# Where the tiles lie in SBUF: large buffers at multiples of 1024 bytes, small ones last

## The chip, the cores and the metric

One NeuronCore of a Trainium2 chip runs the whole program in one launch. The metric is the device time of one execution in microseconds (us). The median of three runs of the kernel before is 3648.97 us (3647.49 to 3654.26).

## What is computed

Two blocks follow each other on 256 tokens of width 1024, all in fp32. The first has two layers of feed-forward (SwiGLU, inner width 2816), a mixer and a second feed-forward. The mixer joins a causal depthwise convolution (31 taps) and differential attention with 4 heads. The second block has one retention mixer, one gated spatial unit, and behind each of them a "PEER" layer: 8 heads pick 16 of 16,384 experts for each token. This is the core of the reference, cut to the parts that carry the time:

```
x = x + 0.5 * swiglu(rms_norm(x, g1), w_gate, w_up, w_down)      # 1024 -> 2816 -> 1024
a, g, q, k, v = split(rms_norm(x, g2) @ w_in)                    # mixer
x = x + concatenate([conv(a, g), diff_attention(q, k, v)]) @ w_out
...
x = x + g1 * retention_mixer(h, ...)      # layer 0 of the second block
x = x + g1 * sgu_mixer(h, ...)            # layer 1 of it
x = x + g2 * peer_ffn(h, ...)             # both layers
# peer_ffn: scores of h @ w_query against sub_keys, top 16 of 128 twice, top 16 of the 256 sums,
#   softmax gates; u = expert_u[idx]; a = gelu(u . x) * gate; out = a . expert_v[idx]
return rmsnorm(x, norm_final)
```

## The kernel before

The activations lie transposed: 8 tiles of 128 channels by 256 tokens. Every large product is done in three passes, since a factor in the matmul's `float32r` type loses bits: each factor is split into a high part (`h_hi`, `w_hi`, `a_hi`, ...) and a low part (the rest, `h_lo`, `w_lo`, ...), and TensorE adds high*high, low*high and high*low. The three are the lines 548, 549 and 550 (`triple`), and 553, 554 and 555 (`loose`, for the PEER layers' second product). The first operand of each call is the stationary one, the 128x128 block that is loaded into the array; the second is the moving one, 256 columns of 4 bytes, or 1024 bytes in each partition. In `project_rows` the roles are swapped and 512 columns of weights move.

The weights stream from HBM. SyncE issues one transfer of 1 MB per pair of "units" into one of three `raw` buffers; for each unit (128x1024) ScalarE writes `w_hi` (line 936), VectorE (line 1316) or, for the PEER queries and first expert table, GpSimd (line 1892) writes `w_lo`, and TensorE uses the pair in 24 matmuls. Four unit slots of `w_hi` and `w_lo` rotate. The order of the work on each engine is written out by hand, and semaphores tie them.

What moves in a matmul is one of these: a slice of `h_hi` or `h_lo`, 256 columns (projections, 3 x 4416 matmuls); a tile of the "arena", whose names are `at...` in the trace, 256 columns (second products, 3 x 1152 at lines 548 to 550, and 3 x 2048 at 553 to 555); or a slice of `w_hi`/`w_lo`, 512 columns (3 x 192).

The partition is filled from the front by `sb`, one buffer behind the other at multiples of 32 bytes. The arena is one large buffer; `place` puts tiles into it at a given offset, and `carve` one behind the other. 16,512 bytes are taken before the first buffer. From the sizes in the code the start of each buffer follows, and its rest when divided by 1024:

```
buffer                      before      rest    after       rest
x                           16512       128     17408       0
h_hi, h_lo                  24704 ...   128     25600 ...   0
raw (3 x 8192 bytes)        51904       704     41984       0
w_hi, w_lo (4 x 4096)       76480 ...   704     66560 ...   0
arena                       109248      704     99328       0
a_hi, rc_hi, z_hi, p_hi...  in arena    704     in arena    0
mixer's cat_hi, cat_lo      in arena    160     in arena    0
```

The tiles of the second row from below lie at multiples of 1024 bytes within the arena already; slices of 256 tokens within any of these keep the rest of the whole. The weights' blocks of 128 columns (512 bytes) start at a rest of 704 or 192 before, and of 0 or 512 after.

Of the kernel before, what the change touches and what calls it, by code (L numbers as in the profile page):

```python
# [9 lines left out]
FR = mybir.dt.float32r  # L10
# [7 lines left out]
T = 256  # L18
# [4 lines left out]
UNIT = 1024  # L23
BLK = 8
NRAW = 3
NPAIR = 4
NEG = -1e30
NRING = 38
NLATE = 5
NI = 32  # L30
# [63 lines left out]
def carver(place, at=0):  # L94

    state = [at]

    def take(*shape, dt=FP):
        v = place(state[0], *shape, dt=dt)
        n = int(np.prod(shape))  # L100
        state[0] += (n if dt is not HF else (n + 1) // 2) + 7 & ~7
        return v

    return take, state


def weight_order(a):
# [3 lines left out]
    def add(key, src, count, lo="v", n0=0):  # L111
        nonlocal n
        for i in range(n0, n0 + count):
            first.setdefault(key, n) if n0 == 0 and i == 0 else None
            order.append((src[i], lo, n))
            place[key, 2 * i], place[key, 2 * i + 1] = n, n + 1
            n += 2
# [19 lines left out]
    def add_peer(l):  # L137
        u, v = a["peer_u"][l], a["peer_v"][l]
        for i in range(8):
            add(("peer_q", l), a["peer_q"][l], 1, "p", i)  # L140
            if i >= 1:
                add(("peer_u", l), u, 1, "p", i - 1)
        add(("peer_u", l), u, NRING // 2 - 7, "p", 7)
        for i in range(64):
            add(("peer_v", l), v, 1, "v", i)
            if i + NRING // 2 < 64:
                add(("peer_u", l), u, 1, "p", i + NRING // 2)

# [12 lines left out]
def build(nc, a, out):  # L161
    ctx = ExitStack()
    with ctx:
        def sb(name, shape, dt=FP):
            return ctx.enter_context(nc.sbuf_tensor(name, shape, dt))[:]

        def signal(name, order=lambda: 1):
            return Signal(ctx.enter_context(nc.semaphore(name)), order)

        x = sb("x", [128, KT, T])  # L170
        hh_ = sb("h_hi", [128, KT, T], FR)
        hl_ = sb("h_lo", [128, KT, T], FR)
        sq = sb("sq", [128, 2, T])
        tmp_h = sb("tmp_h", [128, 3, T])
        ident = sb("ident", [128, 128])
# [10 lines left out]
        gs = sb("gs", [128, L, 16])  # L186
        lam = sb("lam", [128, 20])
        subg = sb("subg", [128, L])
        raw_t = sb("raw", [128, NRAW, 2 * UNIT])
        whi = sb("w_hi", [128, NPAIR, UNIT], FR)  # L190
        wlo = sb("w_lo", [128, NPAIR, UNIT], FR)
        NA = 29000
        arena_at = (nc.sbuf_base + 31) // 32 * 32
        sb("arena", [128, NA])

        def place(at, *shape, dt=FP):
            n = int(np.prod(shape))
            assert at % 8 == 0 and at + (n if dt is not HF else (n + 1) // 2) <= NA
            v = nc.alloc_sbuf_tensor_at(f"at{at}_{nc.next_id()}", [128, n], dt, offset=arena_at + 4 * at)[:]
# [13 lines left out]

        A_BIAS = NA - 4 * 384
        A_TRI = A_BIAS - D - 3 * T
# [225 lines left out]
        carve, end = carver(place)  # L441
# [4 lines left out]
        carve, end = carver(place)  # L446
# [8 lines left out]
        msqa = [carve(2, T) for _ in range(4)]  # L455
        mrs = [carve(2 * T) for _ in range(2)]
        mdiag = [carve(128) for _ in range(4)]
        cat_hi, cat_lo = carve(8, T, dt=FR), carve(8, T, dt=FR)
        msg = [carve(2, T) for _ in range(2)]
        mct = [carve(T) for _ in range(2)]  # L460
# [9 lines left out]
        carve, end = carver(place)  # L470
# [14 lines left out]
        carve, end = carver(place)  # L485
# [14 lines left out]
        carve, end = carver(place)  # L500
        G = [carve(NI // 2, T) for _ in range(3)]
        scratch_end = end[0]
        R = carve(NRING, T)
        p_hi = [carve(T, dt=FR) for _ in range(4)]
# [8 lines left out]
        carve, end = carver(place)  # L513
# [30 lines left out]
        def _(e):  # L544
# [288 lines left out]
            def peer(l):  # L833
# [4 lines left out]
                def u_pair(n):  # L838
                    b = take(ub, ("u", l, n))
                    project(q, unit[("peer_u", l), 2 * n], b[:, 0:T])  # L840
                    project(q, unit[("peer_u", l), 2 * n + 1], b[:, T:2 * T])

                n_u = 0
                for n in range(8):
# [12 lines left out]
                    if n >= 1:  # L857
                        u_pair(n_u)
                        n_u += 1
                for n in range(n_u, NRING // 2 - NLATE):  # L860
                    u_pair(n)
# [15 lines left out]

                late = list(range(NRING // 2 - NLATE, NRING // 2))
                for gg in range(16):
# [1168 lines left out]
```

## Time and profile before

| | |
|---|---|
| median of 3 runs | 3648.97 us |
| the profiled execution | 3643.59 us, span 3641.8 us, mean granted clock 0.951 |
| TensorE matmul busy | 3387.4 us (93%), 28,708 matmuls |
| TensorE weight load busy | 3304.4 us (91%) |
| VectorE busy | 2338.4 us (64%) |
| ScalarE busy | 1668.5 us (46%) |
| GpSimd busy | 847.6 us (23%) |
| moved by DMA | 588.31 MB, mean 162 GB/s |

How to read it: a matmul's busy time runs from its start to its modelled end, and neighbours overlap; so the time that one takes out of the stream is the distance from its start to the next start, which the timeline shows, and not its duration. The granted clock is the share of TensorE's full 2.4 GHz; 0.5 is 1.2 GHz.

### The profile page before, as it was taken

The page shows a single profiled execution, that of the slowest core. Times are in us where ns is not written, and L with a number is a line of the kernel's source. Part 1 is how long each engine was busy: PE and PEld are TensorE (multiplying, and loading weights), DVE is VectorE, ACT ScalarE, POOL GpSimd, SP SyncE. Part 2 cuts the span into 40 slices and gives each one's busy share as a digit, 9 for nine tenths or more (in the row PEclk, how much of TensorE's full clock was granted, in tenths as well). Part 3 has the DMA queues.
Part 4 walks back from the last instruction along what each step waited for, and adds up shares of the span by engine and source line. Part 5 has one row for each costly group of instructions (what it writes and reads, how often), then busy time and mean ns, then how long its engine had stood idle before and what let it go on. Part 6 is the DMA issues. An engine that isn't in the chain of part 4 may idle for free.

```text
span 3641.8 us, 66194 instructions
## 1 busy us (share of the span) xinstructions
PE 3387.4 (93%) x28708; PEld 3304.4 (91%) x28708; DVE 2338.4 (64%) x3670; ACT 1668.5 (46%) x2556; POOL 847.6 (23%) x421
## 2 busy tenths in 40 slices
PE   7996899997799998989999999999987999999999
PEld 7985799996699898979999999989987999999998
DVE  5766586867477655984554736666589546465565
ACT  5444454544544454434444444456443344444444
POOL 0014000006000001662334343000066233433310
PEclk9998899998899999978999999999998799999999
DMA  6651366663166443433445354445444253544433
GB/s 225 232 215 52 119 252 224 252 219 127 55 217 248 174 151 139 151 116 123 156 144 181 129 176 148 151 173 181 163 141 138 82 176 137 174 141 161 163 131 124
DMA packets 82656, 588.31 MB, mean 162 GB/s; under 512 B 9308, under 2 KB 10912, under 8 KB 11712
## 3 DMA queue, kind: packets, MB, share of 16 engines
q1 hardware_dynamic: 80064, 575.70, 45.0%
q10 hardware_dynamic: 1888, 6.94, 0.5%
q8 instruction: 227, 3.72, 0.4%
q0 software_dynamic: 416, 1.45, 0.2%
q14 instruction: 61, 0.50, 0.0%
HBM read 583.00 MB, written 1.05 MB: 160 GB/s over the span
## 4 chain that ended last, share of the span: by engine, by line
PE 80%; DVE 14%; ACT 4%; issue 1%; DMA 0%; ACTq 0%; DVEq 0%
PE ps L548 16%; PE ps L549 16%; PE ps L550 16%; PE ps L875 7%; PE ps L553 7%; PE ps L555 7%; PE ps L554 7%; PE ps L676 2%; DVE at L1726 1%; DVE at L1777 1%; PE ps L600 1%; DVE at L1807 1%; DVE w_lo L1316 1%; ACT w_hi L936 1%; DVE at L1474 1%
## 5 line engine op out<-in xcount | busy, mean ns | idle before, releaser
L936 ACT ACTIVATE w_hi<-raw 128x1024 fp32r<-128x1024 f32 x1000 | 1055.6, 1058 | 851.5 <-PE ps L550 633.3
L1316 DVE TENSOR_TENSOR w_lo<-raw,w_hi 128x1024 fp32r<-128x1024 f32 x712 | 893.2, 1258 | 645.1 <-ACT w_hi L936 644.5
L548 PE MATMUL ps<-h_hi,w_hi 128*128 128x256 f32 x4416 | 1257.1, 285 | 47.7 <-POOL w_lo L1892 33.4
L549 PE MATMUL ps<-h_lo,w_hi 128*128 128x256 f32 x4416 | 1243.9, 282 | 0.0
L550 PE MATMUL ps<-h_hi,w_lo 128*128 128x256 f32 x4416 | 1242.5, 281 | 0.0
L1892 POOL TENSOR_TENSOR w_lo<-raw,w_hi 128x1024 fp32r<-128x1024 f32 x288 | 722.8, 2517 | 1759.8 <-ACT w_hi L936 1759.8
L548 PEld LDWEIGHTS ps<-h_hi,w_hi 128*128 128x128 f32 x4416 | 853.4, 193 | 55.2 <-POOL w_lo L1892 33.8
L549 PEld LDWEIGHTS ps<-h_lo,w_hi 128*128 128x128 f32 x4416 | 854.2, 193 | 0.8 <-issue 0.2
L550 PEld LDWEIGHTS ps<-h_hi,w_lo 128*128 128x128 f32 x4416 | 852.4, 193 | 0.0
L553 PE MATMUL ps<-at,w_hi 128*128 128x256 f32 x2048 | 591.3, 289 | 8.4 <-DVE at L1826 8.4
L555 PE MATMUL ps<-at,w_lo 128*128 128x256 f32 x2048 | 582.6, 284 | 0.0
L554 PE MATMUL ps<-at,w_hi 128*128 128x256 f32 x2048 | 582.6, 284 | 0.0
L553 PEld LDWEIGHTS ps<-at,w_hi 128*128 128x128 f32 x2048 | 398.2, 194 | 9.0 <-issue 9.0
L554 PEld LDWEIGHTS ps<-at,w_hi 128*128 128x128 f32 x2048 | 396.0, 193 | 0.0
L555 PEld LDWEIGHTS ps<-at,w_lo 128*128 128x128 f32 x2048 | 395.7, 193 | 0.0
L548 PE MATMUL ps<-at,w_hi 128*128 128x256 f32 x1152 | 334.1, 290 | 6.6 <-DVE at L1555 3.7
L549 PE MATMUL ps<-at,w_hi 128*128 128x256 f32 x1152 | 328.0, 285 | 0.0
L550 PE MATMUL ps<-at,w_lo 128*128 128x256 f32 x1152 | 327.9, 285 | 0.0
L875 PE MATMUL ps<-at,at 128*128 128x32 f16 x4096 | 293.2, 248 | 14.1 <-DVE at L1807 14.0
L875 PEld LDWEIGHTS ps<-at,at 128*128 128x128 f16 x4096 | 275.7, 163 | 21.0 <-issue 16.4
L1826 DVE TENSOR_TENSOR at<-at,at 128x256 fp32r<-128x256 f32 x256 | 97.6, 423 | 290.8 <-ACT at L1252 290.8
L1801 DVE TENSOR_TENSOR at<-at,at 128x2048 f16<-128x2048 f16 x128 | 209.3, 1635 | 38.4 <-PE ps L875 38.3
(252 smaller groups left out, 3522.6 us busy)
## 6 DMA issues: line engine op xcount, KB each, us to landing
raw<-in_peer_u SPq DMA_DIRECT2D x128, 1024.0 KB, 4.9
raw<-in_peer_v SPq DMA_DIRECT2D x128, 1024.0 KB, 4.9
raw<-in_ffn_gu SPq DMA_DIRECT2D x88, 1024.0 KB, 4.8
raw<-in_ada_w SPq DMA_DIRECT2D x48, 1024.0 KB, 4.8
raw<-in_ffn_down SPq DMA_DIRECT2D x44, 1024.0 KB, 4.8
raw<-in_w_in SPq DMA_DIRECT2D x16, 1024.0 KB, 4.8
raw<-in_peer_q SPq DMA_DIRECT2D x16, 1024.0 KB, 4.9
raw<-in_sgu_v SPq DMA_DIRECT2D x12, 1024.0 KB, 4.8
```

The costliest lines, as they stand in the source:

```text
L548: e.matmul(o, lhs[0], rhs[0], start=start, stop=False)
L549: e.matmul(o, lhs[0], rhs[1], start=False, stop=False)
L550: return e.matmul(o, lhs[1], rhs[0], start=False, stop=stop)
L553: e.matmul(o, lhs[0], rhs[0], start=start, stop=False, skip_group_check=True)
L554: e.matmul(o, lhs[0], rhs[1], start=False, stop=False, skip_group_check=True)
L555: return e.matmul(o, lhs[1], rhs[0], start=False, stop=stop, skip_group_check=True)
L875: t = e.matmul(b[:, k * NI:(k + 1) * NI], Bh[j][:, :, k], Ah[j][:, z, :, k], start=z == 0, stop=z == 1)
L936: e.activation(whi[:, u % NPAIR, :], raw(k, half), ACT.Copy).then_inc(hi_done.hit(u), 1)
L1316: e.tensor_tensor(wlo[:, m % NPAIR, :], raw(k, half), whi[:, m % NPAIR, :].bitcast(FP), ALU.subtract).then_inc(w_lo_dve.hit(m), 1)
L1801: e.tensor_tensor(Bh[j], jT[:, t0:t0 + 16].unsqueeze(1).broadcast_to([128, 128, 16]), iot, ALU.is_equal)
L1826: e.tensor_tensor(p_lo[k % 4], R[:, ir + e2, :], p_hi[k % 4].bitcast(FP), ALU.subtract).then_inc(p_lo_done.hit(l, k), 1)
L1892: e.tensor_tensor(wlo[:, n % NPAIR, :], raw(k, half), whi[:, n % NPAIR, :].bitcast(FP), ALU.subtract).then_inc(w_lo_pool.hit(n), 1)
```

## The change

No instruction is added, removed or moved: on each engine the same operations with the same tiles and shapes stand in the same order. Only addresses differ. A filler of 896 bytes brings the first buffer to a multiple of 1024; `raw`, `w_hi`, `w_lo` and the arena move in front of the small buffers (all of them whole multiples of 1024 bytes long but the arena, which is last of them); and the mixers' concatenated tiles are carved at the next multiple of 256 floats. The small buffers (`sq`, `tmp_h`, `ident`, `ones`, `cols`, `rr` and so on) now follow the arena, from byte 215,328 on.

```
+LINE = 1024
...
+        front = -((nc.sbuf_base + 31) // 32 * 32) % LINE
+        if front:
+            sb("front", [128, front], mybir.dt.uint8)
         x = sb("x", [128, KT, T])
         hh_ = sb("h_hi", [128, KT, T], FR)
         hl_ = sb("h_lo", [128, KT, T], FR)
+        raw_t = sb("raw", [128, NRAW, 2 * UNIT])
+        whi = sb("w_hi", [128, NPAIR, UNIT], FR)
+        wlo = sb("w_lo", [128, NPAIR, UNIT], FR)
+        NA = 29000
+        arena_at = (nc.sbuf_base + 31) // 32 * 32
+        assert arena_at % LINE == 0, (arena_at, front)
+        sb("arena", [128, NA])
         sq = sb("sq", [128, 2, T])
         tmp_h = sb("tmp_h", [128, 3, T])
...
         subg = sb("subg", [128, L])
-        raw_t = sb("raw", [128, NRAW, 2 * UNIT])
-        whi = sb("w_hi", [128, NPAIR, UNIT], FR)
-        wlo = sb("w_lo", [128, NPAIR, UNIT], FR)
-        NA = 29000
-        arena_at = (nc.sbuf_base + 31) // 32 * 32
-        sb("arena", [128, NA])
...
         mdiag = [carve(128) for _ in range(4)]
+        carve, end = carver(place, -(-end[0] // T) * T)
         cat_hi, cat_lo = carve(8, T, dt=FR), carve(8, T, dt=FR)
```

## Rows read from the trace of the kernel before

**Rows 1.** Page, busy time: share of the span and instructions of each engine.

```profile
PE 3387.4 (93%) x28708; PEld 3304.4 (91%) x28708; DVE 2338.4 (64%) x3670; ACT 1668.5 (46%) x2556; POOL 847.6 (23%) x421
```

**Rows 2.** Page, costliest groups: busy us, mean ns | idle before, releaser.

```profile
L548 PE MATMUL ps<-h_hi,w_hi 128*128 128x256 f32 x4416 | 1257.1, 285 | 47.7 <-POOL w_lo L1892 33.4
...
L553 PE MATMUL ps<-at,w_hi 128*128 128x256 f32 x2048 | 591.3, 289 | 8.4 <-DVE at L1826 8.4
...
L548 PE MATMUL ps<-at,w_hi 128*128 128x256 f32 x1152 | 334.1, 290 | 6.6 <-DVE at L1555 3.7
```

**Rows 3.** Timeline, TensorE, first to second PEER product: start us, us; clock 1.0.

```profile
1719.73 0.28 PE L550 MATMUL ps<-h_hi,w_lo 128*128 128x256 f32 x1
...
1721.77 0.28 PE L550 MATMUL ps<-h_hi,w_lo 128*128 128x256 f32 x1
1721.88 0.28 PE L553 MATMUL ps<-at,w_hi 128*128 128x256 f32 x1
...
1723.91 0.28 PE L555 MATMUL ps<-at,w_lo 128*128 128x256 f32 x1
```

**Rows 4.** Timeline, TensorE, clock 1.0: w_out at 408 us, ffn_down at 550 us.

```profile
407.74 0.28 PE L549 MATMUL ps<-at,w_hi 128*128 128x256 f32 x1
...
408.21 0.28 PE L550 MATMUL ps<-at,w_lo 128*128 128x256 f32 x1
...
549.76 0.28 PE L549 MATMUL ps<-at,w_hi 128*128 128x256 f32 x1
...
550.96 0.28 PE L550 MATMUL ps<-at,w_lo 128*128 128x256 f32 x1
```

**Rows 5.** Timeline, TensorE, retention's rows: moving w, 512 columns, clock 1.0.

```profile
1262.03 0.39 PE L548 MATMUL ps<-w_hi,h_hi 128*128 128x512 f32 x1
...
1263.86 0.39 PE L550 MATMUL ps<-w_hi,h_lo 128*128 128x512 f32 x1
```

**Rows 6.** Timeline, TensorE, around 620 and 978 us, clock 0.5.

```profile
619.92 0.41 PE L548 MATMUL ps<-h_hi,w_hi 128*128 128x256 f32 x1
...
621.42 0.41 PE L549 MATMUL ps<-h_lo,w_hi 128*128 128x256 f32 x1
...
978.09 0.41 PE L550 MATMUL ps<-at,w_lo 128*128 128x256 f32 x1
...
979.80 0.41 PE L549 MATMUL ps<-at,w_hi 128*128 128x256 f32 x1
```

**Rows 7.** Timeline, TensorE, a two-pass fp32 product, clock 1.0; its groups row.

```profile
99.57 1.88 PE L647 MATMUL ps<-at,at 128*128 128x512 f32 x4
...
L682 PE MATMUL ps<-at,half 128*128 128x512 f32 x16 | 8.2, 591 | 0.0
```

**Rows 8.** Windows by stage, line 548 alone: us, PE busy (x), clock, DMA share, GB/s.

```profile
1400.00:1535.00 135.00, 87.06 (x300) 0.94 0.44 151
1535.00:1680.00 145.00, 60.71 (x198) 0.78 0.28 95
1680.00:2380.00 700.00, 199.22 (x720) 1.00 0.46 157
...
2755.00:2900.00 145.00, 60.44 (x196) 0.78 0.28 95
```

**Rows 9.** Windows by stage: us, PE, PEld, DVE, ACT, POOL, clock, DMA share, GB/s.

```profile
400.00:530.00 130.00, 126.99 (x1092) 126.83 (x1092) 97.71 (x142) 66.97 (x98) 0.00 (x0) 0.97 0.64 234
530.00:598.00 68.00, 68.00 (x580) 68.00 (x579) 45.77 (x61) 31.77 (x43) 0.00 (x0) 1.00 0.65 235
...
1535.00:1680.00 145.00, 121.06 (x1138) 119.39 (x1137) 113.93 (x170) 49.53 (x85) 63.27 (x25) 0.78 0.28 95
1680.00:2380.00 700.00, 693.91 (x6542) 691.43 (x6542) 398.85 (x490) 309.44 (x468) 220.09 (x88) 1.00 0.46 157
```

**Rows 10.** One line's instructions: duration ns min/median/max; DMA issues, us to landing.

```profile
L1892 POOL TENSOR_TENSOR w_lo<-raw,w_hi x288: 2361/2407/3515, 1417.4 to 3489.7; 128x1024 fp32r<-128x1024 f32 x144
...
raw<-in_ffn_gu SPq DMA_DIRECT2D x88, 1024.0 KB, 4.8
```

**Rows 11.** Page, costliest groups: split of the weights on VectorE.

```profile
L1316 DVE TENSOR_TENSOR w_lo<-raw,w_hi 128x1024 fp32r<-128x1024 f32 x712 | 893.2, 1258 | 645.1 <-ACT w_hi L936 644.5
```

## The prediction

> **What bounds the kernel now.** First the page: TensorE's matmuls are busy for 3387.4 us of the 3641.8 us span, 93%; VectorE comes next with 64% [rows 1]. Then the cut by stages: in the second feed-forward product TensorE is busy for 68.00 of 68 us, in the long PEER stretch for 693.91 of 700, while VectorE is at 67% and 57% there and the DMA engines at 0.65 and 0.46 [rows 9]. Where TensorE waits, it is short in sum (47.7 us ahead of line 548's 4416 matmuls, 8.4 us ahead of line 553's [rows 2]). So in most of the span nothing but TensorE's own stream sets the time, and the question is what one matmul takes out of that stream.
>
> That is read from starts in the timeline. With `h` as the moving operand, 18 slots lie between 1719.73 and 1721.77: 113.3 ns each. Right behind them, with an arena tile moving against the same weight buffers, 17 slots lie between 1721.88 and 1723.91: 119.4 ns [rows 3]. In the feed-forward it is 10 slots in 1.20 us, 120 ns; with the mixer's concatenated tiles 4 slots in 0.47 us, 117.5 ns [rows 4]. With 512 columns of weights moving, 8 slots in 1.83 us, 228.8 ns [rows 5]. 256 columns at 2.4 GHz are 106.7 ns and 512 are 213.3: each wide matmul pays 6.6, 10.8, 13.3 or 15.5 ns on top. At half clock, 7 slots in 1.50 us and 8 in 1.71 us are 214 ns each, for `h` and for the concatenated tiles alike, against 213.3 for 256 columns at 1.2 GHz [rows 6]. So what comes on top isn't a fixed part of the instruction; it shows only when the columns are read at the full rate, and it depends on which buffer moves.
>
> Beside the addresses it has an order: a start with a rest of 128 by 1024 costs 6.6 ns, 160 costs 10.8, 704 (192 by 256 or by 512) costs 13.3. Counted in cycles of 2.4 GHz that is 272, 282 and 288; with the starts taken by 256, 128, 160 and 192 bytes are 32, 40 and 48 elements, and 240 plus that count gives 272, 280 and 288. Three points on a line, and at rest 0 the line would be under the 256 cycles that the columns need. The stationary blocks start at 704 or 192 in all but the 512-column case, and make no difference among these.
>
> **The change part by part.** No instruction moves, so no wait, queue or transfer changes its place; there are only durations to reprice.
>
> Wide matmuls with `h` moving, rest 128 to 0. There are 3 x 4416 = 13,248 [rows 2]. I take out those in the two stretches where the expert matrix G begins to be built (1535 to 1680 and 2755 to 2900 us), since there VectorE is busy for 113.93 of 145 us and TensorE's stream waits on it and on GpSimd [rows 9]: 3 x (198 + 196) = 1182 [rows 8]. Of the remaining 12,066 some stand in half-clock time, where nothing is to be gained; with clocks of 0.94 to 1.00 in the stages that hold them [rows 8, 9], and half-clock time mostly around waits, I count 2.5% off: 11,760.
>
> Wide matmuls with arena tiles: 3 x (2048 + 1152) = 9600 [rows 2], nearly all at clock 1.00; 3% off: 9310. Weights moving, 512 columns: 3 x 192 = 576, with 3% off 560.
>
> The new slot isn't in the trace; no wide moving operand starts at a whole 1024. The lower bound is the columns alone, 106.7 ns. An upper bound is the best that is seen now, 113.3 ns; above that only if the alignment itself hurts (below). The nearest row for a floor is a two-pass fp32 product, which reads at half the rate: 4 starts and one duration of 591 ns in 1.88 us make (1.88 - 0.591) / 3 = 429.7 ns for the 426.7 ns of 512 half-rate columns, 3.0 ns on top [rows 7]; rounding makes that 2 to 3. I take 2 ns: 108.7 ns, and 215.4 ns for 512 columns.
>
> Then `h` gains 11,760 x (113.3 - 108.7) = 54 us; the arena tiles 9310 x (120 - 108.7) = 105 us (the 384 concatenated ones count 2.5 ns less each, 1 us in all: 104 us); the weights 560 x (228.8 - 215.4) = 7.5 us. The sum is 166 us. At the lower bound of 106.7 ns it is 78 + 123 + 9 = 210 us; at the upper bound 0 + 60 + 4 = about 64 us (for the weights half of the gain).
>
> The Trainium skill, "TensorE: Matmul & The Clock Gate", section "Wait — 56ns, not 53.3ns?", gives the slot as N / 1.2 at the low clock and N / 2.4 + 2.5 ns at the high one. The first agrees with this trace (214 ns); the second would be 109.2 ns for 256 columns, and no row at full clock is that short (113.3 at best). By that rule as the slot at rest 0 the sum would be 48 + 100 + 7 = 155 us.
>
> What lies beside: GpSimd's split is 2407 ns per unit [rows 10] and a unit's 24 matmuls go from 24 x 113.3 = 2719 to 2609 ns, so it stays hidden by 0.2 us where it is alone; it is late where VectorE works on two inputs as well (its worst is 3515 ns), which is in the stretches that I took out. VectorE's split (1258 ns, [rows 11]) with a stage's other work fills 97.71 of 130 us in ffn_gu [rows 9]; TensorE's 127 us there shrink by about 5 to 122, so 80%. In ffn_down the DMA engines go from 0.65 to about 0.71 of their time, and a transfer of 1 MB, 4.8 us from issue to landing [rows 10], has two and more units' time (over 5.2 us each pair) in three buffers. So the cover stays, thinner. VectorE, ScalarE and GpSimd aren't repriced: I take 0 for them, since their operations with the same shape take the same at any start (the split's three operands at rest 704 are the only long ones, and their spread in the trace goes with GpSimd's work beside them). If they gained or lost 5%, it would be behind TensorE in the long stages and cost or give at most some 10 us in the chains of the mixers and of the top-16 search.
>
> From the profiled execution's 3643.59 us: 3643.6 - 166 = 3477.6. The median of the runs shown lies 5.4 us above it: 3483 us.
>
> **The rivals.** Slower: a clash of equal starts. Before, where the moving and the stationary block have the same rest by 512 (192 and 192), the slot is 120; where they lie 64 bytes apart (128 and 192) it is 113.3; at 32 bytes apart (160 and 192) 117.5. That order fits a clash of two reads as well as it fits the start of the moving one. After the change all of them are at 0, and `h` would pay as the arena tiles do: 11,760 x 6.7 = 79 us more, 3728 us. It would decide from the first projection on. Against it: where weights move and `h` is stationary they are 64 bytes apart too, and yet 512 columns pay 15.5 ns and not 6.6 [rows 5]. I give it 7%.
>
> No change: what differs between `h` and the arena isn't the start but the place or the neighbours' traffic. For it: VectorE writes the arena at the same time, and all starts are multiples of 32 bytes already. Against it: the 120 ns hold in three stages with different neighbours, the 113.3 ns stand right beside them. The Trainium skill, "SBUF — State Buffer", in the table at its head ("Cachelines"), has lines of 16 bytes, and by that rule every operand here is aligned and the change is worth nothing: 3649 us. The trace speaks against it by the 6.7 ns. I give it 5%.
>
> Only the best of today: 113.3 ns is what a read at full rate costs whatever its start, and only the worse starts improve. Then 64 us are gained: 3649 - 64 = 3585 us. For it: nothing in the trace is shorter, and the slot is the same against both rests of the weights. Against it: the line through three points, and the half-clock rows. I give it 10%.
>
> **How the numbers follow.** My forecast (slot between 106.7 and 110.5 ns) has 78%, the clash 7%, no change 5%, the best of today 10%. Alone, the forecast reaches from 3649 - 215 = 3434 to 3649 - 125 = 3524 us. Toward the third rival the range is opened to 3570, which leaves out the clash, no change, and part of the third; the low end is set to 3430. Less than 0.2% (7 us) can't be told from no change in this kernel. Faster by more than that: 88%; within it: 5%; slower: 7%.
>
> **What will show it.** In the changed kernel's timeline the starts of line 548 to 550 with `h` moving and those of 553 to 555 must have the same distance, under 111 ns; mean durations of both groups in the groups part must be equal and about 5 ns (`h`) and 11 ns (arena) lower. The half-clock slots must stay at 214 ns. The two PEER stretches of some 700 us must lose about 40 us each, the mixers' stretches (204 to 400 and 790 to 990 us) only 2 to 5. VectorE's split must still take about 1258 ns. I'm wrong if `h` goes to 120 ns, if the two groups stay apart, or if the idle time of TensorE ahead of line 548 grows by tens of us, with GpSimd's or VectorE's split as its releaser.

## The result: slower by 1.6%

The changed kernel takes 3708.34 us (median of 4 runs, 3707.05 to 3711.4) against 3648.24 us for the kernel before (4 runs): ratio 1.0162, with a 95% interval of 1.0145 to 1.018, or some 60 us more. The forecast was 3483 us with a range of 3430 to 3570; the sign is wrong. It went the way of the first rival, the clash of equal starts, which had been given 7% and a time of 3728 us.

The profiled execution has a span of 3705.2 us at a mean granted clock of 0.954 (before: 3641.8 at 0.951), so the granted clock isn't what cost the time. The change put six more lines ahead of the engines' code: line 554 is what was 548, 559 what was 553, 1322 what was 1316 and 1898 what was 1892. First the page's busy time and costliest groups (busy us, mean ns | idle time before, releaser):

```profile
PE 3458.7 (93%) x28708; PEld 3375.2 (91%) x28708; DVE 2345.8 (63%) x3670; ACT 1667.4 (45%) x2556; POOL 845.1 (23%) x421
...
L554 PE MATMUL ps<-h_hi,w_hi 128*128 128x256 f32 x4416 | 1280.3, 290 | 44.1 <-POOL w_lo L1898 31.2
...
L559 PE MATMUL ps<-at,w_hi 128*128 128x256 f32 x2048 | 592.2, 289 | 8.4 <-DVE at L1832 8.4
...
L1322 DVE TENSOR_TENSOR w_lo<-raw,w_hi 128x1024 fp32r<-128x1024 f32 x712 | 892.6, 1257 | 675.2 <-ACT w_hi L942 675.1
```

TensorE is busy for 71.3 us more [rows 1]. The mean matmul with `h` moving went from 285 to 290 ns, the one with an arena tile stayed at 289 [rows 2]. VectorE's split takes 1257 ns [rows 11: 1258]. GpSimd's, from the view of one line (ns: least/median/most), is 2407 at the median in both [rows 10]:

```profile
L1898 POOL TENSOR_TENSOR w_lo<-raw,w_hi x288: 2374/2407/3517, 1449.4 to 3553.4; 128x1024 fp32r<-128x1024 f32 x144
```

Now the slots. TensorE's timeline (start us, modelled length us) in the first PEER layer, `h` moving at clock 1.0; the stretch that answers to the first part of [rows 3]:

```profile
1754.75 0.28 PE L554 MATMUL ps<-h_hi,w_hi 128*128 128x256 f32 x1
1754.87 0.28 PE L555 MATMUL ps<-h_lo,w_hi 128*128 128x256 f32 x1
1754.99 0.28 PE L556 MATMUL ps<-h_hi,w_lo 128*128 128x256 f32 x1
...
1758.35 0.28 PE L554 MATMUL ps<-h_hi,w_hi 128*128 128x256 f32 x1
```

30 slots in 3.60 us: 120.0 ns, where they were 113.3. With an arena tile moving there are 34 slots in 4.08 us, 120.0 ns. The 119.4 ns that the prediction read in the second part of [rows 3] held the first slots behind `h`, of which some are shorter; the settled slot was 120 ns before too, as in the feed-forward [rows 4]:

```profile
1724.87 0.28 PE L559 MATMUL ps<-at,w_hi 128*128 128x256 f32 x1
...
1728.95 0.28 PE L560 MATMUL ps<-at,w_hi 128*128 128x256 f32 x1
```

With 512 columns of weights moving, 10 slots in 2.27 us are 227 ns, a little *less* than the 228.8 of [rows 5]:

```profile
1294.05 0.39 PE L554 MATMUL ps<-w_hi,h_hi 128*128 128x512 f32 x1
...
1296.32 0.39 PE L555 MATMUL ps<-w_lo,h_hi 128*128 128x512 f32 x1
```

And at half clock nothing changed; 8 slots in 1.71 us are 214 ns (213.3 by the unrounded starts), as in [rows 6]:

```profile
633.35 0.41 PE L555 MATMUL ps<-h_lo,w_hi 128*128 128x256 f32 x1
...
635.06 0.41 PE L554 MATMUL ps<-h_hi,w_hi 128*128 128x256 f32 x1
```

Where the time lies is seen by windows between the same instructions of both kernels (us, PE, PEld, DVE, ACT, POOL, clock, DMA share, GB/s): in the first line the second feed-forward product (ffn_down, layer 0) with the last 19 us of the `h` products ahead of it, in the others the two long PEER stretches.

```profile
542.80:611.90 69.10, 69.10 (x581) 69.10 (x580) 45.53 (x60) 31.59 (x43) 0.00 (x0) 1.00 0.64 229
1715.50:2429.80 714.30, 709.08 (x6544) 706.45 (x6543) 398.62 (x490) 308.92 (x468) 218.63 (x89) 1.00 0.45 154
...
2950.40:3664.00 713.60, 708.38 (x6529) 705.75 (x6528) 397.58 (x489) 307.69 (x467) 220.09 (x88) 0.99 0.45 154
```

The first PEER stretch took 700 us in [rows 9] and takes 714.3 now; it holds 3 x 720 matmuls with `h`, and their starts lie 12.6 us further apart in all, 0.9 us are at the arena's matmuls and 0.7 us at the rest. The window around ffn_down took 68.1 us and takes 69.1, but this 1.0 us belongs to the 161 `h` matmuls at its front; from the first matmul of ffn_down, where only arena tiles move, to its last (548.2 to 614.1 us before) it is 65.9 us before and 65.8 after. Stage by stage:

```
stage (start before, us)         before   after    h 64 off (e8)
feed-forward up (400)             130.0   135.9    135.8
feed-forward up (598)             124.0   129.8    129.9
mixers (204 / 790)                196.0 / 200.0   200.3 / 203.3   199.7 / 203.3
retention (1184)                  216.1   219.0    219.1
G built (1535 / 2755)             145.0 / 145.1   144.9 / 140.7   144.9 / 140.7
PEER long (1680 / 2900)           700.1 / 699.9   714.3 / 713.6   714.2 / 713.6
gated unit (2380)                 240.0   240.1    240.1
```

The stretches that aren't listed take 17.4 us more together.

Over the whole trace I take the distances between neighbouring starts under 150 ns, for wide matmuls at full clock, and sort them by the buffers of their operands. Before, `h` moving has a mean of 113.9 ns and arena tiles one of 119.8; after, 120.0 and 119.8. Both traces hold the same 28,708 matmuls in the same order, so the 63.4 us between the spans can be split matmul by matmul, by the distance from each start to the next (the stretches in which G begins to be built have a line of their own and are in no other):

```
11,702 slots with h, full clock                               +70.3 us (6.0 ns each)
9254 slots with arena tiles, full clock                        +0.2
555 slots with 512 columns                                     -1.1
distances behind an h matmul that hold a wait, full clock      -5.2
the two stretches in which G begins to be built                -4.4
all the rest                                                   +3.5
```

Nearly all that the G stretches gave back lies in the second one, 145.1 to 140.7 us, and there the granted clock was 0.82 where it had been 0.78 [rows 8]. That is enough to account for those 4.4 us: 116 of that stretch's `h` matmuls ran at half clock before and 54 after, and 62 slots of 120 instead of 214 ns are 5.8 us. In the gated unit 13 `h` matmuls ran at half clock before and none after, and its `h` slots, too, cost nothing. Why the clock fell less often there isn't shown.

TensorE alone in the second of the G stretches in the changed kernel (us, busy, clock, DMA share, GB/s):

```profile
2809.60:2950.40 140.80, 117.99 (x1135) 0.82 0.28 98
```

### The profile page after: what moved, and what is told of

Read it like the earlier page. It is cut to its first block, busy times and chain, and to the rows that moved or that the text cites. A ratio compares the mean times of both kernels' runs of the same rounds, so it can differ in the third digit from the quotient of the medians.

```text
span 3705.2 us, 66194 instructions
## 1 busy us (share of the span) xinstructions
PE 3458.7 (93%) x28708; PEld 3375.2 (91%) x28708; DVE 2345.8 (63%) x3670; ACT 1667.4 (45%) x2556; POOL 845.1 (23%) x421
## 4 chain that ended last, share of the span: by engine, by line
PE 81%; DVE 14%; ACT 3%; issue 1%; DMA 0%; ACTq 0%; DVEq 0%
PE ps L554 17%; PE ps L555 16%; PE ps L556 16%; PE ps L881 7%; PE ps L559 7%; PE ps L560 7%; PE ps L561 7%; PE ps L682 2%; DVE at L1732 1%; DVE at L1783 1%; DVE w_lo L1322 1%; ACT w_hi L942 1%; PE ps L606 1%; DVE at L1813 1%; DVE at L1807 1%
## 5 line engine op out<-in xcount | busy, mean ns | idle before, releaser
L554 PE MATMUL ps<-h_hi,w_hi 128*128 128x256 f32 x4416 | 1280.3, 290 | 44.1 <-POOL w_lo L1898 31.2
L1322 DVE TENSOR_TENSOR w_lo<-raw,w_hi 128x1024 fp32r<-128x1024 f32 x712 | 892.6, 1257 | 675.2 <-ACT w_hi L942 675.1
L555 PE MATMUL ps<-h_lo,w_hi 128*128 128x256 f32 x4416 | 1267.5, 287 | 0.0
L556 PE MATMUL ps<-h_hi,w_lo 128*128 128x256 f32 x4416 | 1266.3, 287 | 0.0
L554 PEld LDWEIGHTS ps<-h_hi,w_hi 128*128 128x128 f32 x4416 | 866.8, 196 | 51.6 <-POOL w_lo L1898 31.6
L555 PEld LDWEIGHTS ps<-h_lo,w_hi 128*128 128x128 f32 x4416 | 867.1, 196 | 0.9 <-issue 0.2
L556 PEld LDWEIGHTS ps<-h_hi,w_lo 128*128 128x128 f32 x4416 | 865.7, 196 | 0.0
```

The source lines that it names most:

```text
L554: e.matmul(o, lhs[0], rhs[0], start=start, stop=False)
L555: e.matmul(o, lhs[0], rhs[1], start=False, stop=False)
L556: return e.matmul(o, lhs[1], rhs[0], start=False, stop=stop)
L1322: e.tensor_tensor(wlo[:, m % NPAIR, :], raw(k, half), whi[:, m % NPAIR, :].bitcast(FP), ALU.subtract).then_inc(w_lo_dve.hit(m), 1)
```

## The experiments

From here on I speak of a *distance*: the start of the moving slice less the start of the stationary block, in bytes, by 256. Before the change it was -64 for `h` (128 against 192), 0 for the arena (192 against 192), -32 for the concatenated tiles, and +64 where 512 columns of weights move; after it, 0 for all. The prediction had named the rests 704 and 192 of the stationary blocks as different; by 256 they are the same. The experiments are told by question and not in the order in which they ran.

### Is it `h` alone?

e8, on the kernel before: every buffer keeps its rest but `h`, which moves from rest 128 to 704, and so to distance 0.

```
+        sb("gap0", [128, 576], mybir.dt.uint8)
         hh_ = sb("h_hi", [128, KT, T], FR)
         hl_ = sb("h_lo", [128, KT, T], FR)
+        sb("gap1", [128, 448], mybir.dt.uint8)
```

> One part of the change alone: the kernel before, in which only h_hi and h_lo are moved so that they start with the same rest as w_hi and w_lo (704); fillers keep x, raw, w and the arena at their rests. Theory A: h goes from 113.9 to 120 ns, arena unchanged at 120, total as after the change, 3708 us. If instead the new place of the small buffers, raw or x cost the time, this stays at 3648 us.

3708.85 us, ratio 1.016 [1.0144, 1.0177]: the whole loss. The stages agree with those of the changed kernel within 0.6 us each (last column of the table above), and the slot is 120.0 ns (timeline: 22 slots in 2.64 us; then the group):

```profile
1754.75 0.28 PE L550 MATMUL ps<-h_hi,w_hi 128*128 128x256 f32 x1
...
1757.39 0.28 PE L551 MATMUL ps<-h_lo,w_hi 128*128 128x256 f32 x1
...
L550 PE MATMUL ps<-h_hi,w_hi 128*128 128x256 f32 x4416 | 1279.7, 290 | 44.1 <-POOL w_lo L1894 31.2 <-DVE h_lo L1360 7.6 <-DVE w_lo L1318 5.3
```

So the other parts of the change (`raw`, `x`, the small buffers behind the arena, the concatenated tiles) are together worth nothing that can be measured in the total. The concatenated tiles, which stay at distance -32 in e8 (118.4 ns) and are at 0 in the changed kernel (119.3 ns), make 0.1 us in each mixer.

### Is it the start of the moving slice, or its distance from the stationary block?

e4, on the kernel before: `h` stays at rest 128, where the prediction's law has 113.3 ns; only `w_hi` and `w_lo` move, to rest 640, which is 128 by 256.

```
+        sb("gap0", [128, 960], mybir.dt.uint8)
         whi = sb("w_hi", [128, NPAIR, UNIT], FR)
         wlo = sb("w_lo", [128, NPAIR, UNIT], FR)
+        sb("gap1", [128, 64], mybir.dt.uint8)
```

> The kernel before (h at rest 128, arena at 704, that is 192 by 512), in which only w_hi and w_lo move from rest 704 to 640 (128 by 512). Theory A: the moving h and the stationary block now start alike, so h goes from 113.3 to 120 ns; the arena tiles start 64 bytes behind the stationary block and leave 120 ns (113 if the sign of the distance doesn't count). Theory B: h stays at 113.3 ns and the arena at 120, total 3648 us.

3693.74 us, ratio 1.0111 [1.0055, 1.0166]. `h`, unmoved, went from 113.9 to 119.9 ns; the arena, unmoved too but now at distance +64, from 119.8 to 117.8 ns. In the groups:

```profile
L550 PE MATMUL ps<-h_hi,w_hi 128*128 128x256 f32 x4416 | 1278.7, 290 | 44.2 <-POOL w_lo L1894 31.3 <-DVE h_lo L1360 7.6 <-DVE w_lo L1318 5.3
...
L555 PE MATMUL ps<-at,w_hi 128*128 128x256 f32 x2048 | 587.2, 287 | 8.4 <-DVE at L1828 8.4
```

That ends the law of the prediction: a buffer that didn't move changed its slot. The stationary start alone doesn't decide either: with it at 192 by 256, `h` at 128 had 113.9 ns and the arena at 192 had 119.8, both in the kernel before. The distance decides: +64 makes 117.8 ns from starts 192 and 128 (here) and from 0 and 192 (e1, below), and 0 makes 119.8 to 120.0 from starts 192 and 192, 128 and 128, 0 and 0. The 512-column matmuls, for which the distance also became 0, went to 227.0 ns here as in the changed kernel.

### What does each distance cost?

For this the four unit slots of the weights, in the changed kernel, were given starts of their own, so that one run measures four distances with `h` and the arena at rest 0:

```
+SHIFT = (0, 64, 128, 192)          # bytes; e2: 256, 320, 384, 448; and so on
+whi_t = sb("w_hi", [128, NPAIR * UNIT + 256], FR)
+def slot(t, n):
+    at = n % NPAIR * UNIT + SHIFT[n % NPAIR] // 4
+    return t[:, at:at + UNIT]
```

> The changed kernel, in which the four unit slots of w_hi and of w_lo start at rests of 0, 64, 128 and 192 bytes (unit n uses slot n modulo 4); all moving h and arena tiles stay at rest 0. Theory A (only the distance between the moving block's start and the stationary block's counts, modulo 512): slots of 120 ns for units at 0, about 113.3 ns at 64, and less at 128 and 192 if the line through 32 and 64 bytes goes on (106.7 to 109 ns). Theory B (only the moving block's own start counts, and 128 happens to be good): 120 ns for all four, total 3708 us. With A the total is 3708 less a share of each slot: about 3708 - 5300 x (6.7 + 12 + 12) ns = 3545 us.

> As before, the four slots at rests of 256, 320, 384 and 448. Theory A: distances of 256 to 448 bytes; if the effect has a period of 256 bytes this repeats the run with 0 to 192 (120, 113, and two below); if it has one of 512 bytes, 256 and 320 are as good as 192 and the last rises again towards 120. Theory B: 120 ns for all, 3708 us.

> As before, the four slots at rests of 32, 96, 160 and 224. Theory A: 117 ns at 32, 110 at 96, 107 to 109 at 160; at 224 the same, or 117 again if the period is 256 bytes. Theory B: 120 ns for all, 3708 us.

> The changed kernel with the four slots of w_hi and w_lo at rests of 48, 56, 72 and 80 bytes. Theory A with a smooth dependence: 115 and 114 ns at 48 and 56, and 114 and 115 at 72 and 80 or still less; if 64 bytes are a step of a line and only whole multiples count, these four fall apart (116 to 119). Total between 3590 and 3680 us.

> The changed kernel with the four slots of w_hi and w_lo at rests of 16, 112, 208 and 240, the rest of the map. If only whole multiples of 64 bytes have a short settled pattern, these lie between 116.5 and 120 ns and the total at 3680 us; if there is a short pattern beside 64 bytes, one of the four lies under 115 ns.

Measured: e1 3678.32 us, 1.0056 [1.0036, 1.0076]; e2 3676.29, 1.0061 [1.004, 1.0081]; e3 3683.59, 1.0079 [1.0054, 1.0104]; e7 3674.73, 1.0066 [1.0042, 1.0089]; e10 3678.54, 1.0069 [1.0042, 1.0096]. The mean slots over all units of a kind, with the weights' rest ahead of the moving slice's by

```
bytes   0     16    32    48    56    64     72    80    96    112
ns     119.9 118.5 118.4 118.2 117.8 116.0* 118.4 118.8 118.7 119.7
bytes  128   160   192   208   224   240
ns     118.6 119.8 117.8 116.8 116.8 117.5
```

(The 119.9 at 0 is of units between others; in the changed kernel, where all stand at 0, it is 120.0.) e2 repeats e1 within 0.1 ns at its four distances, so 256 bytes is the period. The curve isn't a line: theory A, which let the line go on past 64 bytes, had e1 at 3545 us. The prediction's three points (0, 32, 64 ahead) were points of this curve, and its middle one was low: the concatenated tiles have a mean of 118.3 ns over the whole product around 408 us, not the 117.5 that four slots of it gave [rows 4], and 118.4 is what 32 bytes ahead make here. Within a stream the slots settle in a pattern that then repeats. For instance e1's timeline, in a unit at distance 0, where slots of 121, 120, 124, 118 and 117 ns follow each other in this order over and over (the view rounds the starts to 10 ns):

```profile
450.21 0.28 PE L560 MATMUL ps<-h_hi,w_hi 128*128 128x256 f32 x1
450.33 0.28 PE L561 MATMUL ps<-h_lo,w_hi 128*128 128x256 f32 x1
450.45 0.29 PE L562 MATMUL ps<-h_hi,w_lo 128*128 128x256 f32 x1
450.58 0.28 PE L560 MATMUL ps<-h_hi,w_hi 128*128 128x256 f32 x1
450.70 0.28 PE L561 MATMUL ps<-h_lo,w_hi 128*128 128x256 f32 x1
450.81 0.28 PE L562 MATMUL ps<-h_hi,w_lo 128*128 128x256 f32 x1
```

The value with the star is a mixture. At distance -64 (64 bytes ahead) there are *two* patterns: 113, 113, 114 ns (short) and 118, 117, 118 ns (long). Of 231 runs of 15 slots at -64 in e1, 94 have a mean of 114 and 137 of 118. At the fifteen other distances of the four runs e1, e3, e7 and e10 nearly none has a mean under 116: 3 of 236 at +64, of some 3,400 in all.

### What do -64 everywhere, and the arena's own -64, give?

e5, on the changed kernel: SHIFT is 64 for all four slots, so `h` and the arena both stand at -64. e6, on the kernel before: `sb("gap1", [128, 960], mybir.dt.uint8)` ahead of the arena brings it to rest 640, and so to -64, where `h` is already.

> The changed kernel with all four slots of w_hi and w_lo 64 bytes further on, so that every moving tile (h, arena, concatenated) starts 64 bytes before the stationary block by 256; x, h, raw and the arena stay at rest 0. Theory A (the distance decides, and 64 bytes ahead is the good one): all wide slots at 113.3 to 114 ns. Against the changed kernel's 120 that is 6.3 ns on some 21,000 matmuls, about 120 us less than 3708, so 3590 us. Theory C (what was good in the kernel before is the absolute start of h at 128, and the map of distances only shows a disturbance of it): 116 to 120 ns, 3640 to 3700 us.

> The kernel before with one filler of 960 bytes ahead of the arena, so that the arena moves from rest 704 to 640 and its tiles start 64 bytes before the stationary block; everything else keeps its address. Theory A: line 553 to 555 and the arena's part of 548 to 550 go from 120 to 113.7 ns, some 9000 x 6.1 ns = 55 us less, 3595 us; h unchanged at 113.9. Theory C: no change, 3648 us.

e5: 3623.33 us (3621.69 to 3634.34), 0.9923 [0.9907, 0.994]. e6: 3633.93, 0.9954 [0.9936, 0.9972]. Both are faster than the kernel before, but by less than 113.3 ns for every matmul would give: 9310 x 6.5 ns = 61 us, and e5 gained 27. Their mean slots are 115.3 (`h`) and 115.8 ns (arena) in e5, 115.2 and 116.2 in e6. The slots say why. Two stretches of e5's timeline at clock 1.0, with the same operands:

```profile
119.83 0.28 PE L560 MATMUL ps<-h_hi,w_hi 128*128 128x256 f32 x1
...
122.32 0.28 PE L561 MATMUL ps<-h_lo,w_hi 128*128 128x256 f32 x1
...
449.72 0.28 PE L561 MATMUL ps<-h_lo,w_hi 128*128 128x256 f32 x1
...
452.31 0.28 PE L562 MATMUL ps<-h_hi,w_lo 128*128 128x256 f32 x1
```

22 slots in 2.49 us are 113.2 ns; 22 in 2.59 us are 117.7. A stream keeps the pattern with which it starts: of the pairs of units with `h` that follow each other without a break at full clock, 372 in the kernel before, 372 in e5 and 374 in e6, not one changed its pattern between the two. In e5 the feed-forward streams from 423 and 618 us (1034 and 1035 matmuls without a break) are in the long one from end to end. The arena can reach the short one as well, as in e6 (22 slots in 2.49 us):

```profile
559.82 0.28 PE L550 MATMUL ps<-at,w_hi 128*128 128x256 f32 x1
...
562.31 0.28 PE L551 MATMUL ps<-at,w_lo 128*128 128x256 f32 x1
```

The kernel before had both as well, which the prediction missed. Its first feed-forward, from 101.4 us on, runs 479 matmuls in the long one (10 slots in 1.18 us):

```profile
121.31 0.28 PE L550 MATMUL ps<-h_hi,w_lo 128*128 128x256 f32 x1
...
122.49 0.28 PE L548 MATMUL ps<-h_hi,w_hi 128*128 128x256 f32 x1
```

But wherever `h` came directly behind an arena stream at distance 0, at full clock, it went into the short one, in 90 of 90 cases. In e5 and e6 there are no such streams at 0 any more: 62 and 61 of the 90 go into the long one, and `h` is worse than before by 1.3 to 1.4 ns. Of the runs of 15 slots at distance -64, 73 of 806 have the long pattern in the kernel before, and 647 of 1355 in e5.

### Can the short pattern be forced?

e11 puts three matmuls at distance 0 into each unit of a projection: e5's placing, and the last of the eight tiles of `h_hi` and `h_lo` lies 64 bytes further on. (Here the weights come to rest 64 by the 64 bytes more behind `h_lo`, and a filler of 960 bytes brings the arena back to 0.)

```
+        hh_t = sb("h_hi", [128, KT * T + 256], FR)
+        hl_t = sb("h_lo", [128, KT * T + 16], FR)
+        def tile(t, m):
+            at = m * T + (16 if m == KT - 1 else 0)
+            return t[:, at:at + T]
```

> As the run with all of w 64 bytes ahead (3623 us), but the last of the eight h tiles, high and low, lies 64 bytes further on, at distance 0, so that each unit of h products holds three matmuls that settle differently. In the trace of the run before, the distance of 64 bytes has two settled patterns, 113, 113, 114 ns and 118, 117, 118 ns; a stream keeps the one it starts with for up to 1000 matmuls. Theory R (three matmuls at distance 0 bring the stream into the pattern of 113, as the arena's do in the kernel before): h at 114.5 ns on average, some 0.8 ns less than 115.3, total 3610 us. Theory S (they throw it into either pattern): h at 116 to 118, total 3630 to 3660 us.

3606.69 us (5 runs, 3599.33 to 3608.86), 0.9876 [0.986, 0.9893]: 41 us faster than the kernel before, 102 faster than the changed one, and the best of all versions that ran. One unit of the stream that had the long pattern in e5; the shifted tile's three matmuls begin at 441.01, 441.36 is outside it again:

```profile
441.01 0.28 PE L560 MATMUL ps<-h_hi,w_hi 128*128 128x256 f32 x1
...
441.36 0.28 PE L560 MATMUL ps<-h_hi,w_hi 128*128 128x256 f32 x1
...
441.71 0.28 PE L560 MATMUL ps<-h_hi,w_hi 128*128 128x256 f32 x1
...
443.75 0.28 PE L560 MATMUL ps<-h_hi,w_hi 128*128 128x256 f32 x1
```

3 slots in 0.35 us (116 ns by the unrounded starts), then after 3 more 18 slots in 2.04 us, 113.3 ns; 24 in 2.74 us, 114.2 ns for the unit, where the long pattern makes 2.82. Over the trace 131 of 1059 runs of 15 slots at -64 have the long pattern (647 of 1355 in e5); `h` has 114.1 ns (116.3 in the shifted tile) and the arena 114.4. That the three matmuls do it is seen from unit to unit: of 31 units in the long pattern that the next one follows directly, 23 are followed by one in the short pattern, and of 343 in the short pattern none by a long one. So the shifted tile puts a stream right most of the time, not always. In the groups:

```profile
L560 PE MATMUL ps<-h_hi,w_hi 128*128 128x256 f32 x4416 | 1262.2, 286 | 47.7 <-POOL w_lo L1904 32.9 <-DVE h_lo L1370 7.6 <-DVE w_lo L1328 7.1
...
L565 PE MATMUL ps<-at,w_hi 128*128 128x256 f32 x2048 | 582.1, 284 | 8.4 <-DVE at L1838 8.4
```

Against e5 the first feed-forward streams fell from 133.5 to 130.6 (400 us) and from 128.0 to 125.2 us (598 us), and the long PEER stretches from 700.3 and 699.3 to 687.5 and 688.0.

### Which block counts, and is 113.3 ns a floor?

During a matmul the next stationary block is being loaded (in the kernel before, matmuls are busy for 93% of the span and loads for 91% [rows 1]). So the distance that counts could be the one to the matmul's own block or the one to the next. e9, on e5: `w_lo` moves back by 64 bytes to distance 0 while `w_hi` stays at -64; of the three passes one has its own block at 0 and another has the next one at 0.

```
+def slot(t, n, less=0):
+    at = n % NPAIR * UNIT + SHIFT[n % NPAIR] // 4 - less     # w_lo: less=16
```

> The changed kernel with w_hi at rest 64 and w_lo at rest 0, moving tiles at 0. Theory A1 (the moving read meets the load of the next stationary block): of the three passes only the second, high weights with the low moving tile, is followed by a block at distance 0, so its slot is the long one and the other two are short. Theory A2 (it meets its own stationary block): the third pass, whose own block is at distance 0, is the long one. Theory A3 (the sequence settles as a whole): all three differ from what each distance gives alone, mean over the three between 115 and 120 ns. Total about 3640 to 3690 us in each.

3681.66 us, 1.0081 [1.0058, 1.0104]. The passes have a mean of 118.2 ns (own block `w_hi`, next `w_hi`), 118.8 (own `w_hi`, next `w_lo`) and 117.5 (own `w_lo`, next `w_hi`): neither one alone decides, and a stream settles at 118, 117, 118 as a whole (timeline: 21 slots in 2.47 us, 117.6 ns):

```profile
449.89 0.28 PE L562 MATMUL ps<-h_hi,w_lo 128*128 128x256 f32 x1
...
452.36 0.28 PE L562 MATMUL ps<-h_hi,w_lo 128*128 128x256 f32 x1
```

e12, e13 and e14 change the size of the stationary block instead: the stationary block of the expert table `u` has 64 (or 32) of its 128 columns. They leave out the outputs of the other experts, so each of these matmuls also writes only 64 (or 32) of its 128 output rows. The number of loads, the moving columns and all other work stay.

```
-def project(q, n, o):                 +def project(q, n, o, rows_=128):
-    c = slice(k * 128, (k + 1) * 128) +    c = slice(k * 128, k * 128 + rows_)
-    triple(o, ...)                    +    triple(o[0:rows_], ...)
     project(q, unit[("peer_u", l), 2 * n], b[:, 0:T], 64)      # e14: 32
```

> The changed kernel (all at rest 0, slot 120 ns) in which the first expert product (peer_u, 3 x 2048 matmuls) loads only 64 of each block's 128 stationary columns and so computes only 64 of the 128 experts of a block; the other 64 rows keep what the bank held. The moving read is unchanged. Theory L (what comes on top of 106.7 ns is the meeting of the moving read with the read of the stationary block): with half the load the slot falls from 120 to about 107 to 113 ns in those products, total down by 6144 x 7 to 13 ns, 3630 to 3665 us. Theory M (the moving read alone loses it, at each start): 120 ns stays, 3708 us.

> The first expert product with half the stationary columns (64 of 128 experts of a block computed, as in the run before), now with all of w 64 bytes ahead. Theory P (what is left at the distance of 64 bytes, 6.6 ns, is still the meeting with the load): with half the load the u products go under 112 ns, towards 106.7. Theory F (6.6 ns are a floor of the full-rate read): they stay at 113 to 114 ns, as with half the load at distance 0.

> The changed kernel (distance 0), the first expert product with 32 of 128 stationary columns (32 of the 128 experts of a block computed). Theory P: the slot goes on falling with the load, 120 at 128 columns, 113.5 at 64, 107 to 111 at 32. Theory F: it stays at 113.3 ns, the floor.

One execution each: e12 (distance 0, 64 columns) 3673.49 us beside 3647.79 of the kernel before; e13 (distance -64, 64) 3629.4 and e14 (distance 0, 32) 3694.03, both beside 3653.27. e12's timeline, and after it the groups by form:

```profile
1751.91 0.28 PE L554 MATMUL ps<-h_hi,w_hi 128*64 128x256 f32 x1
...
1753.83 0.28 PE L556 MATMUL ps<-h_hi,w_lo 128*64 128x256 f32 x1
1753.95 0.28 PE L559 MATMUL ps<-at,w_hi 128*128 128x256 f32 x1
...
1754.43 0.28 PE L560 MATMUL ps<-at,w_hi 128*128 128x256 f32 x1
...
L554 PE MATMUL ps<-h_hi,w_hi 128*64 128x256 f32 x2048 | 573.4, 280 | 32.7 <-POOL w_lo L1898 32.7
...
L554 PEld LDWEIGHTS ps<-h_hi,w_hi 128*64 128x64 f32 x2048 | 279.1, 136 | 33.2 <-POOL w_lo L1898 33.2
```

At distance 0 the halved load takes the slot from 120 to 113 ns (17 in 1.92 us), and the arena tile right behind it, with whole loads, is at 120 again (4 in 0.48 us). So the size of the stationary block matters at distance 0. Whether it acts through the load, whose mean is 136 ns here and 197 in the whole blocks of the other products with `h`, or through the output rows, which were halved with it, these runs don't separate. Nor is smaller simply better. In e14 the same groups read

```profile
L554 PE MATMUL ps<-h_hi,w_hi 128*32 128x256 f32 x2048 | 582.9, 285 | 31.7 <-POOL w_lo L1898 31.7
...
L554 PEld LDWEIGHTS ps<-h_hi,w_hi 128*32 128x32 f32 x2048 | 225.9, 110 | 50.5 <-POOL w_lo L1898 32.2
```

and the slots have a mean of 116.4 to 117.0, worse than with 64 columns: 63 of 245 units run at 113 ns and 182 at 118, where in e12 all but one of 248 run at 113. In e13 blocks of 64 columns at -64 make 116.6, some units at 113 and the others at 118 to 120; neither of its two theories (under 112 ns, or 113 to 114) came true. In no kernel that ran did any stream settle under 113.3 ns.

## Why the prediction was wrong

**The bound was right.** TensorE's stream set the time: of the 14.2 us more in the long PEER stretch, 12.6 are the slots of `h`. Nothing else had to be repriced: the splits took 1257 and 2407 ns, the half-clock slots 214, and TensorE's waits didn't grow.

**The step that failed** is the law: "it depends on which buffer moves", with "the stationary blocks start at 704 or 192 ..., and make no difference among these". They had the same rest by 256, so the kernel before never varied them, and three points on a line in the moving start were three distances from one stationary start. e4 shows it with a buffer that didn't move, e8 with one that did. So `h`, which was to gain 54 us, lost 70.3, and the arena tiles, which were to gain 104 us, gave 0: their distance was 0 and is 0.

**The rival that was right** was argued away with [rows 5]: at 512 columns the operands lie 64 bytes apart and pay 15.5 ns all the same. That is true, and e4 and the changed kernel show that it says nothing of 256 columns: for 512 the distance 0 is the *better* one (227.0 against 229.0 ns). I had carried a row across a change of width and of sign (+64, not -64). Its price of 79 us was 11,760 x 6.7; measured are 6.0 ns on 11,702 slots, since 113.3 is the short pattern and not the mean. Some 7 of these 70.3 us were given back elsewhere, so the spans differ by 63.4 and the medians by 60.

**The floor of 108.7 ns** rested on [rows 7], a product that reads at half the rate. At half clock the slot is 213 to 214 ns at distances -64, -32 and 0 alike, so a slow read says nothing of the full-rate one; for the two-pass product itself no run varied the distance. No kernel here came under 113.3 ns. Even with the right distance known, the third rival's 64 us for all wide matmuls at 113.3 ns would have been the most to be had by the settled slots seen here; e11 reached 41 of it.

By the Trainium skill, "TensorE: Matmul & The Clock Gate", section "Wait — 56ns, not 53.3ns?", the slot would be 109.2 ns at the high clock; the lowest settled slot of any run is 113.3 ns, and for 512 columns 227 against the 215.8 that this rule of the Trainium skill makes. The low-clock rule of the Trainium skill agrees with the traces (213 to 214 ns). By the 16-byte lines of the Trainium skill, "SBUF — State Buffer", table at its head ("Cachelines"), all multiples of 16 would be equal; among those of e10 and e3 the means lie 3.0 ns apart (116.8 to 119.8).

**What stays open** is the mechanism. Shown are the dependence on the distance by 256 bytes, the two patterns at -64 and that a stream keeps its own, and that a smaller stationary block changes the slot at distance 0. Whether that is its load or its fewer output rows, why 64 columns are better than 32, which of two neighbouring blocks counts, and whether the phase in which a stream starts can be set by hand, is not settled; a kernel with all loads from one block and moving slices at every distance wasn't tried.

## What to carry over

- Read slots from start to start, over whole streams and sorted by the addresses of *both* operands; a quantity that never varied in the trace (here the stationary start by 256 bytes) can't be ruled out by it.
- For 256 `float32r` columns with a 128x128 block at full clock, let the moving slice lie 64 bytes before the stationary block by 256; aligning all buffers alike (distance 0, 119.9 to 120.0 ns) is, with the block 112 or 160 bytes ahead (119.7 and 119.8), the dearest of the placings measured.
- Look at whole streams: one at -64 may hold 117.7 ns for a thousand matmuls, and a few matmuls at distance 0 in each unit put it back to 113.3 in 23 of 31 cases. In this kernel -64 everywhere brought 3650 to 3623 us, and these few matmuls 3607.

## What the hardware showed beyond that

The stream has a memory: with equal instructions, operands' distance and clock it runs in one of two patterns, 113.3 or 117.7 ns, and each was kept for over 1000 matmuls (1035 in the long one in e5, 1044 in the short one from 622 us in the kernel before). And where TensorE waits and its clock falls, slower `h` slots can cost nothing: in the second stretch in which G begins to be built they came with fewer matmuls at half clock (54 with `h` for 116; e8 has 54 as well, e4 29) and with 4.4 us less. What the clock followed there isn't shown.
